# Strassen's seven products in eight of ten feed-forward down-projections of a fp32 transformer kernel

## What is computed

```python
# first block, D_FF = 4096
h = rmsnorm(x, norm_ffn[l])
x = x + jnp.square(jax.nn.relu(h @ w_ff1[l])) @ w_ff2[l]

# second block, two layers, D_FF_2 = 2816
def conv_ffn(xn, w_up, conv_w, w_down):
    up = xn @ w_up
    a, g = jnp.split(up, 2, axis=-1)
    a = causal_dwconv(a, conv_w)
    return (jax.nn.silu(a) * g) @ w_down
```

## Time and profile before

| | us |
|---|---|
| median of 3 runs | 2031.22 |
| lowest, highest | 2030.95, 2031.37 |
| the profiled execution, first to last instruction | 2029.2 |
| PE busy in it | 2022.2 |
| DVE busy | 993.0 |
| ACT busy | 795.4 |
| POOL busy | 870.7 |

### The profile page before, as it was taken

How to read it: one execution, slowest core, us unless ns; L and a number is a source line. 1 busy time by engine, 2 the same in 40 slices (tenths; PEclk the granted TensorE clock), 3 DMA queues, 4 the chain that set the end, 5 groups by cost and what they waited for, 6 DMA issues and landing times.

```text
span 2029.2 us, 25410 instructions
## 1 busy us (share of the span) xinstructions
PE 2022.2 (100%) x10270; PEld 1659.3 (82%) x10270; DVE 993.0 (49%) x1502; ACT 795.4 (39%) x1144; POOL 870.7 (43%) x357
## 2 busy tenths in 40 slices
PE   9999999999999999999999999999999999999999
PEld 7888888888888888888888888888877778888887
DVE  4688888634221314434463242454377746334142
ACT  6455556534222224512432222246377743223222
POOL 4334443644444444444444444453422234444444
PEclk9999999999999999999999999999999999999999
DMA  5222222442333332323333333333311123323323
GB/s 179 83 84 74 84 84 84 130 134 94 104 94 104 94 94 94 104 94 91 96 94 104 94 94 104 94 115 93 96 61 57 59 76 94 104 91 98 100 93 114
DMA packets 55270, 194.38 MB, mean 96 GB/s; under 512 B 6129, under 2 KB 6641, under 8 KB 55153
## 3 DMA queue, kind: packets, MB, share of 16 engines
q1 hardware_dynamic: 55152, 192.75, 30.6%
HBM read 190.62 MB, written 2.10 MB: 95 GB/s over the span
## 4 chain that ended last, share of the span: by engine, by line
PE 98%; DVE 1%; DMA 0%; SPq 0%; issue 0%; ACT 0%; DVEq 0%
PE ps L1399 30%; PE ps L1400 30%; PE ps L1401 30%; PE ps L1766 1%; PE ps L1732 1%; PE ps L1757 1%; PE ps L1689 1%; PE ps L1691 1%; PE ps L1690 1%; PE ps L1539 1%; PE ps L1407 0%; PE ps L1437 0%; PE ps L1561 0%; DMA w_raw<-in_panels 0%; PE ps L1563 0%; PE ps L1548 0%
## 5 line engine op out<-in xcount | busy, mean ns | idle before, releaser
L355 POOL TENSOR_TENSOR w_lo<-w_raw,w_hi 128x1024 fp32r<-128x1024 f32 x353 | 870.5, 2469 | 1146.5 <-ACT w_hi L374 1118.8
L1399 PE MATMUL ps<-a_hi,w_hi 128*128 128x512 f32 x1472 | 580.9, 395 | 0.3 <-DVE x L848 0.2
L1401 PE MATMUL ps<-a_hi,w_lo 128*128 128x512 f32 x1472 | 573.6, 390 | 0.0
L1400 PE MATMUL ps<-a_lo,w_hi 128*128 128x512 f32 x1472 | 573.3, 389 | 0.0
L374 ACT CAST w_hi<-w_raw 128x1024 fp32r<-128x1024 f32 x353 | 366.0, 1041 | 326.2 <-PE ps L1401 289.5
L1399 PE MATMUL ps<-b_hi,w_hi 128*128 128x512 f32 x1176 | 458.5, 390 | 0.3 <-DVE x L848 0.2
L1401 PE MATMUL ps<-b_hi,w_lo 128*128 128x512 f32 x1176 | 457.6, 389 | 0.0
L1400 PE MATMUL ps<-b_lo,w_hi 128*128 128x512 f32 x1176 | 457.5, 389 | 0.0
L814 DVE TENSOR_TENSOR arena<-ps,inv_rms 128x512 f32<-128x512 f32 x200 | 138.0, 690 | 407.8 <-PE ps L1401 384.4
L1399 PEld LDWEIGHTS ps<-a_hi,w_hi 128*128 128x128 f32 x1472 | 276.3, 188 | 60.5 <-issue 2.8
L1400 PEld LDWEIGHTS ps<-a_lo,w_hi 128*128 128x128 f32 x1472 | 276.4, 188 | 58.1 <-issue 2.2
(11 more groups left out here) (208 smaller groups left out, 1622.7 us busy)
## 6 DMA issues: line engine op xcount, KB each, us to landing
w_raw<-in_panels SPq DMA_DIRECT2D x353, 512.0 KB, 3.5
x<-in_xT SPq DMA_DIRECT2D x16, 256.0 KB, 2.9
outT<-x SPq DMA_DIRECT2D x7, 256.0 KB, 3.8
consts<-in_const SPq DMA_DIRECT2D x1, 528.5 KB, 8.0
arena<-in_rows SPq DMA_DIRECT2D x1, 256.0 KB, 4.5
arena<-in_ws SPq DMA_DIRECT2D x1, 256.0 KB, 5.0
outT<-x SPq DMA_DIRECT2D x2, 128.0 KB, 1.8
consts<-in_late SPq DMA_DIRECT2D x1, 168.0 KB, 2.7
```

What stands on the lines that cost most here:

```text
L355: nc.gpsimd.tensor_tensor(w_lo[:, p % RING, :], w_raw[:, p % RING, :], w_hi[:, p % RING, :].bitcast(F), ALU.subtract).then_inc(w_low, 1)
L1399: nc.tensor.matmul(o, wh, hi[:, kt, :], start=(kt == 0), stop=False)
L1400: nc.tensor.matmul(o, wh, lo[:, kt, :], start=False, stop=False)
L1401: ins = nc.tensor.matmul(o, wl, hi[:, kt, :], start=False, stop=(kt == tiles - 1))
```

## The change

In eight of the ten down stages (`FOLDED`: three of four in `ff1`, two of three in `ffn_0`, all three in `ffn_1`) panels are taken in pairs. A pair is a 2x2 block product: two panels (128 output features each) by two halves of the hidden tiles, times two halves of the hidden tiles by two halves of the positions (256 columns). In place of eight block products of k2 = tiles/2 tiles, seven are made (a form of Strassen's method). For them

- DVE makes four sums of weights from the two raw panels (`sum_weights`): S3, S1, S2, S4. S3, S2, S4 go to PSUM banks, from which ACT makes high and DVE low parts (`high_of_sum`, `low_of_sum`) in single buffers `s_hi`, `s_lo`. S1 overwrites half of the second raw panel and goes through `high` and `low` with it;
- the hidden tiles are turned into sums too, once a stage: T1 in place of half of tiles 0 to k2-1 (`t1`), T2 and T3 (`t2_t3`), T4 (`t4`), each with high and low parts. In the first block the low parts of tiles 4 to 7 themselves are made by POOL (`rest_low_of`);
- PE runs seven blocks of 3 x k2 matmuls of 256 columns (`block` in `down_pairs`). Blocks 1, 4 and 7 go to half a bank in turn, 4 and 7 accumulating on it; DVE adds it into `x` after each (`add_first`, `add_second`, `add_third`), so block 4 waits for `add_first` and block 7 for `add_second`. The four others have half banks of their own (`add_sides`, `add_crossing`).

Every weight panel is loaded as before. Line numbers of the kernel after: L1010, L1012, L1015, L1017 are S3, S1, S2, S4; L1023 `low_of_sum`; L1079 `add_first`; L1087 and L1088 `add_sides`; L1095 `add_second`; L1103 `add_crossing`; L1112 `add_third`; L1047 `t2_t3`; L1055 `t4`; L1060, L1065, L1070 low parts of the hidden tiles. The pieces of the diff are, in this order, the weights' sums, `down_pairs` of DVE, that of ACT, and the body of PE's loop over pairs.

```diff
+            def sum_weights(q, tiles, part):
...
+                if part == 0:
+                    if q > 0:
+                        dve.wait_ge(s_low, 3 * q)
+                    for n in (p, p + 1):
+                        dve.wait_ge(w_in[n % RING], 16 * (n // RING + 1))
+                    v.tensor_tensor(s3, a11, a21, ALU.subtract).then_inc(s_made, 1)
+                    dve.wait_ge(s_made, 4 * q + 1)
+                    v.tensor_tensor(a21, a21, a22, ALU.add).then_inc(s_made, 1)
+                else:
+                    dve.wait_ge(s_made, 4 * q + 2)
+                    v.tensor_tensor(s2, a21, a11, ALU.subtract).then_inc(s_made, 1)
+                    dve.wait_ge(s_made, 4 * q + 3)
+                    v.tensor_tensor(s4, a12, s2, ALU.subtract).then_inc(s_made, 1)
...
+            def down_pairs(key):
+
+                p0, tiles = down_stage(*key)
+                for j in range(DT // 2):
+                    q = PAIR_AT[p0 + 2 * j]
+                    more = j < DT // 2 - 1
+                    if j > 0:
+                        low_of_sum(q, 2, tiles)
+                        add_third(p0, j - 1)
+                    if more:
+                        sum_weights(q + 1, tiles, 0)
+                    if j > 0 or key[0] != "ff1":
+                        add_first(p0, j)
+                    if more:
+                        sum_weights(q + 1, tiles, 1)
+                    add_sides(p0, j)
+                    add_second(p0, j)
+                    if more:
+                        low_of_sum(q + 1, 0, tiles)
+                        low_of_sum(q + 1, 1, tiles)
+                    add_crossing(p0, j)
+                add_third(p0, DT // 2 - 1)
...
+            def down_pairs(key):
+
+                p0, tiles = down_stage(*key)
+                for j in range(DT // 2):
+                    p = p0 + 2 * j
+                    high(p + FEED)
+                    high(p + FEED + 1)
+                    if j < DT // 2 - 1:
+                        for i in range(3):
+                            high_of_sum(PAIR_AT[p + 2], i, tiles // 2 * P)
...
+                    pe.wait_ge(w_low, p + 1)
+                    pe.wait_ge(evicted, p - (1 if j == 0 else 2))
+                    block(acc, a11, lambda kt: (hi[:, kt, 0:HALF], lo[:, kt, 0:HALF]), True,
...
+                    pe.wait_ge(w_low, p + 2)
+                    pe.wait_ge(side_read, 2 * q)
+                    block(p5, s1, lambda kt: (hi[:, kt, HALF:SEQ], lo[:, kt, HALF:SEQ]), True,
...
+                    block(p2, a12, lambda kt: (hi[:, k2 + kt, 0:HALF], lo[:, k2 + kt, 0:HALF]), True,
+                          (lambda kt: (rest_low, rest0 + kt + 1)) if start else None)
+                    pe.wait_ge(s_low, 3 * q + 1)
+                    pe.wait_ge(acc_read, 2 * q + 1)
+                    block(acc, s2, lambda kt: (t23_hi[:, kt, 0:HALF], t23_lo[:, kt, 0:HALF]), False,
...
+                    pe.wait_ge(s_low, 3 * q + 2)
+                    if j > 0:
+                        pe.wait_ge(evicted, p - 1)
+                    block(p3, s4, lambda kt: (hi[:, k2 + kt, HALF:SEQ], lo[:, k2 + kt, HALF:SEQ]), True)
+                    block(p4, a22, lambda kt: (t4_hi[:, kt, :], t4_lo[:, kt, :]), True,
...
+                    pe.wait_ge(s_low, 3 * q + 3)
+                    pe.wait_ge(acc_read, 2 * q + 2)
+                    block(acc, s3, lambda kt: (t23_hi[:, kt, HALF:SEQ], t23_lo[:, kt, HALF:SEQ]), False)
```

More of the change, by code:

```diff
@@ L45, with down_stage @@
 N_PANELS = len(ORDER)
+HALF = SEQ // 2
+FOLDED = [("ff1", 0), ("ff1", 1), ("ff1", 2)] + [(f"ffn_{_l}", _n) for _l in range(2) for _n in range(3) if (_l, _n) != (0, 2)]
+def down_stage(name, n):
+    if name == "ff1":
+        return START["ff1"] + 16 * n + DT, DT
+    return START[name] + 2 * sum(FF2_CHUNKS[:n + 1]) + DT * n, FF2_CHUNKS[n]
+PAIR_AT, TILES_AT, PAIRS = {}, {}, []
+for _name, _n in FOLDED:
+    _p0, _tiles = down_stage(_name, _n)
+    for _m in range(0, DT, 2):
+        PAIR_AT[_p0 + _m] = len(PAIRS)
+        PAIRS.append(_p0 + _m)
+    TILES_AT[_name, _n] = _tiles
+PAIR_OF = {}
+for _p in PAIRS:
+    PAIR_OF[_p], PAIR_OF[_p + 1] = (PAIR_AT[_p], 0), (PAIR_AT[_p], 1)
+WHOLE = [sum(1 for _i in range(_p + 1) if _i not in PAIR_OF) for _p in range(N_PANELS)]
+B1_HIGH, T_HIGH, PART_LOW, REST_LOW = {}, {}, {}, {}
+_b = _t = _l = _r = 0
+for _key in FOLDED:
+    _k2 = TILES_AT[_key] // 2
+    B1_HIGH[_key], T_HIGH[_key], PART_LOW[_key], REST_LOW[_key] = _b, _t, _l, _r
+    _b, _t, _r = _b + 2 * _k2, _t + 3 * _k2, _r + _k2
+    _l += 4 * _k2
 LEVEL_GROUPS = ((0, 1), (2, 3), (4, 5), (6,))
@@ L645, in ffn @@
                         high(p + FEED + 1)
+                        if key in FOLDED and m == size - 1:
+                            for i in range(3):
+                                high_of_sum(PAIR_AT[p + 2], i, k2 * P)
                         act.wait_ge(hid_raw, m + (raw0 + t0 + 1))
-                        split((b_hi if l else a_hi)[:, m, :], conv_o[:, m % 2, :]).then_inc(hid_high, 1)
+                        if key in FOLDED:
+                            high_tile(key, m, keep[m] if m < k2 else conv_o[:, m % 2, :], hi)
+                            high_sums(key, m, conv_o[:, m % 2, :], hi)
+                        else:
+                            split(hi[:, m, :], conv_o[:, m % 2, :]).then_inc(hid_high, 1)
                     p0 += 2 * size
                     t0 += size
-                    if n == len(FF2_CHUNKS) - 1 and l == 0:
+                    if key in FOLDED:
+                        down_pairs(key)
+                    elif n == len(FF2_CHUNKS) - 1 and l == 0:
                         residual(p0, S_ATTN1, "kv", B)
@@ new lines, in add_third @@
+            def add_third(p0, j):
+                q, m = PAIR_AT[p0 + 2 * j], 2 * j
+                dve.wait_ge(part_made, 7 * q + 7)
+                dve.wait_ge(evicted, p0 + m + 1)
+                if p0 + m + 2 < N_PANELS:
+                    both = x[:, m + 1, :].rearrange("p (a n) -> p a n", a=2)
+                    v.tensor_tensor(both, both, acc_of(p0, j).unsqueeze(1).broadcast_to([P, 2, HALF]),
+                                    ALU.add).then_inc(evicted, 1)
+                    return
+                for part in range(2):
+                    at = slice(part * HALF, (part + 1) * HALF)
+                    v.tensor_tensor(x[:, m + 1, at], x[:, m + 1, at], acc_of(p0, j), ALU.add).then_inc(evicted, 1)
@@ L1218, in ffn @@
                                  [gain(f"conv_{l}", m + (t * FF2_TILES + t0)) for t in range(3)]).then_inc(conv_done, 1)
+                        if key in FOLDED and m == size - 1:
+                            q = PAIR_AT[p + 2]
+                            sum_weights(q, size, 0)
+                            sum_weights(q, size, 1)
+                            for i in range(3):
+                                low_of_sum(q, i, size)
                         scale_out(conv_t[:, j, :], p + 1).then_inc(evicted, 1)
@@ L1657, in ffn @@
                     p0 += 2 * size
-                    linear(p0, DT, *hid, hid_low, (HID_FFN1 if l else HID_FFN0) + t0, tiles=size)
+                    if (f"ffn_{l}", n) in FOLDED:
+                        down_pairs((f"ffn_{l}", n), hid)
+                    else:
+                        linear(p0, DT, *hid, hid_low, HID_FFN0, tiles=size)
                     p0 += DT
```

283 lines of the change are left out of this document (264 added, 19 removed).

## The result

The changed kernel takes 2128.9 us (median of 4 runs, 2127.8 to 2129.5) against 2031.1 for the kernel before, a ratio of 1.0481 with a 95% interval of 1.0466 to 1.0496. The forecast was 2111 within 2032 to 2150, slower with a chance of 83%. The profiled execution spans 2127.4 us, 98.2 more than before's 2029.2.

What follows compares the result with a forecast made beforehand. TensorE, busy 2022.2 of 2029.2 us, was taken to bound the kernel. Middle pairs +11.2, last -9.5, first +65.5 and the 6-tile stage +12.7 made +80 on the 2031.2 median: 2111 us, range 2032 to 2150.

Steps and rivals of the forecast that it cites:

- The mechanism: On DVE: instructions with two SBUF inputs do not run beside GpSimd's subtraction and end 0.55 us behind it.
- the middle pairs: Pairs j = 1 and 2 of 8-tile stages: L1079 held behind blocked L1010, block 4 at 6.2, pair 11.7 us, +0.8 each.
- The clash as a whole: All DVE waits for GpSimd: with blocking the sum is +80, 2111 us; without it the same order gives 0, 2031.
- the order alone: Rival: same DVE order with no blocking by GpSimd, stage starts eating the whole gain; 2031 us, chance 8%.
- TensorE's term: Half-width matmuls start 0.1133 us apart (ends 0.112 and 0.120): an 8-tile pair takes 9.52 instead of 10.88, -42 us altogether.
- First pairs behind the convolution: Four stages of 8 tiles: DVE's chain brings L1079's end to 13.9, the pair lasts 19.4 us, +8.5 each.
- The clock: Rival: TensorE loses its clock in 11 new first-pair gaps, 2.7 us more behind each, adding 30; 2141 us, chance 15%.
- the rule that the prediction cited against itself: For TensorE: an idle array falls to half rate until busy again; no row in the body showed that.
- First pairs of the first feed-forward: Three stages: L1095 ends at 20.4, block 7 waits for it since 16.1, the pair lasts 21.4 us, +10.5 each.
- The 6-tile stage: Same chain before shorter blocks: first pair +9.9, middle +1.9 twice, last -1.0, together +12.7 us; unblocked +2.3.
- The rival of 188 ns: Rival: weight loads bound the narrow matmul at 188 ns, +4.9 us in each of 28 pairs; 2183 us, chance 3%.
- What would show it: Signs: TensorE idle about 120 us, put down to DVE at eight stage starts; matmuls 0.113 apart; middle pairs 11.7, last 9.5.

Runs made afterwards that it cites:

- Experiments 1: Changed kernel, but in the pairs' panels GpSimd subtracts only 64 of 1024 columns, leaving most low parts stale; 2062.6 us.
- Experiment 2: Changed kernel with GpSimd whole, but the three weight sums with two SBUF inputs given only one (other sums, same instruction count and order); 2064.6 us.
- experiment 10: Changed kernel with the activations' differences T1 to T4 and their high and low parts made for 32 columns only; 2095.6 us.
- Experiment 5: Changed kernel with GpSimd's low parts cut to 64 columns throughout the paired stages, up panels and its share of the activations included; 2051.3 us.
- experiment 6: Kernel before, with the down panels of the same eight stages made in two passes of 256 columns, nothing else changed; 2059.7 us.
- Experiment 4: Changed kernel with extra 256-column matmuls into an unused bank keeping TensorE busy before the waits in first pairs; 2122.1 us.
- experiment 7: Changed kernel with DVE reordered: evictions TensorE waits for stand ahead of weight sums that can wait, same work and values; 2073.6 us.
- experiment 3: Changed kernel with block 1's addition moved ahead of the next pair's first weight sums, except in the first feed-forward's first pairs; 2089.7 us.
- experiment 9: Changed kernel with evictions reordered, weight sums made through PSUM, and GpSimd's low parts cut to 64 columns in the paired stages; 2048.3 us.

## Why the prediction was right, point by point

- *The mechanism and the middle pairs.* Forecast 11.7 with block 4 at 6.2; measured 11.8 and 6.03. L1010 starts 0.21 behind GpSimd and ends 0.55 behind it, as the earlier trace rows had it for L1222. Experiments 1, 2 and 10 confirm the cause from three sides.
- *The clash as a whole.* The sum had 80 us for it (2111 against 2031 for the order alone). Experiment 5 takes it away and wins 77.6; that this is so near to 80 is in part luck, since the edit also shortens GpSimd's low parts, for which TensorE waited 33.4 us. Experiment 2, which frees the sums alone and leaves GpSimd whole, wins 64, and that is the clean measure for the sums.
- *TensorE's term, mis-sized.* I took 0.1133 between half-width matmuls, half of the earlier trace rows, with 0.120 as the far end. Measured are 0.119 in the last pairs and 0.120 in experiment 6. The earlier trace rows had shown it, 0.11 to 0.12 apart, and I held, 128 columns, for nearer. A pair costs 84 x 0.0057 = 0.5 us more, 15 us in 31 pairs' worth: last pairs take 9.98 in place of 9.52, and the whole gain on TensorE is 27 us instead of 42.
- *First pairs behind the convolution, 19.4 forecast, 21.5 to 22.5 measured.* In the pair shown (22.3) L1079 ended at 14.16 against the 13.9 of the sum; some 0.3 us are the matmuls' distance in the four blocks behind it, and 2.35 are blocks 4 and 5 at a clock of 0.50 and 0.52. The clock was a rival of 15%, with 2.7 us for each of 11 gaps; it is real but smaller. Experiment 4 gives back 8.6 us in these four pairs, and 7 in all on balance. In the first feed-forward most of it falls before a wait that is there anyway (block 7, at 20.5). In the body of the kernel before the granted clock never fell, and there TensorE had no such gap. Here the rule that the prediction cited against itself ("TensorE: Matmul & The Clock Gate", Part 1, of the Trainium skill) agrees with the trace: behind the gap of 3.87 us the array ran at half rate, then at full.
- *First pairs of the first feed-forward.* 21.4 forecast, 22.0 to 23.0 measured, by the two errors above. Block 7 waited for L1095 until 20.48, forecast 20.4.
- *The 6-tile stage.* +12.7 forecast, +11.4 measured; the first pair was 16.65 and not 18.1, the middle ones +1.8 each as forecast.
- *The order without the clash, forecast 2031.* Experiment 5 is the nearest to it and gives 2051. By the lengths of its pairs the eight first ones take 39 us more than before and all the others 20 less. Of the 20 us over the forecast 15 are the matmuls' distance; the rest is not taken apart by a run (the half-rate blocks in the first pairs and the waits there, less what shorter low parts gave). The sentence that even without the clash the stage starts eat the whole gain was right, and too mild.
- *The loads.* The rival of 188 ns is out: loads that last 0.19 stand 0.12 apart. The way in which the prediction turned the Trainium skill's "Trainium Kernel Development and Optimization", Performance Expectations, into a time would have given 2183, 54 us too much. The page gives the share of loads as a measure, beside one of the work done, and no distance between loads. Here loads were busy for 81% of the changed kernel's span without being the limit.
- *What would show it:* TensorE's idle time was to grow to about 120 us; it grew to 92, in part since half-rate blocks count as busy. It was to be put down to DVE; 33.4 us of it are put down to GpSimd, whose low part for block 2 of every first pair (27.0 us) the sum did not have. In the changed kernel that wait hardly adds to a pair's length, since block 4 or 7 waits longer for DVE behind it; in experiment 7, with these waits shortened, it is the largest one left (27.8 us).

What stays open: which gaps cost the clock. Behind the 1.55 us of the 8-tile middle pairs it never fell. But in the 6-tile first pair of experiment 10 it was 0.73 behind a gap of 1.55; in experiment 3 block 7 ran at 1.00 behind gaps of 3.1; a gap of 2.25 did or didn't in the same place (experiment 4), and 1.96 did in one stage of experiment 9 and not in the next. The length of the last gap alone does not tell. It was not tried to begin a stage with two plain panels and pair the other six, which would give the differences time; it needs the activations' plain parts kept beside the differences. With pairs at 9.98 a stage would win 3 x 0.9 = 2.7 us by it, some 21 us in all as an estimate, if nothing else came late. None of the versions run beats the kernel before; the nearest, 2048.3 us, leaves most of GpSimd's low parts out, and the best that makes them all takes 2069.4.

## What to carry to other kernels

Price a saving in arithmetic against the pitch that its smaller pieces really have and against the first use behind each stage start: here one product in eight was 27 us, and eight starts with late operands cost 89 us in the changed kernel (34.8 + 45.3 + 8.5) and still 35 in the freest version. Before work goes to DVE, look which of its instructions take two SBUF operands while GpSimd works, and put what TensorE waits for ahead of them, or bring one operand through PSUM: the order alone gave back 55 us, at no cost.
